# Three of GpSimd's four weight operations in each attention head wait for a named point of VectorE's order

## The reference, cut to what matters

```python
def diff_attention(...):                       # 8 heads, each with two score maps
    ...
    s = jnp.einsum('bhcqd,bhckd->bhcqk', qb, k) * scale
    s = jnp.where(mask, s, -jnp.inf)
    p = jax.nn.softmax(s, axis=-1)
    w = p[:, :, 0] - lam * p[:, :, 1]
    return jnp.einsum('bhqk,bhke->bhqe', w, vv)

def s5_branch(...):                            # linear recurrence over the positions
    ...
    _, states = lax.associative_scan(combine, (a, bu), axis=0)
    y = jnp.einsum('ghp,lbgp->blgh', c, states).real
```

## Time and profile before

| | |
|---|---|
| median of 3 runs | 2371.65 us (2371.1 to 2377.44) |
| the profiled execution, its own time | 2360.77 us |
| its span in the profile | 2359.1 us |
| mean granted TensorE clock | 0.97 |
| busy over the span | PE 93%, PEld 76%, DVE 46%, ACT 43%, POOL 35% |
| the heads' bodies 0 to 6 | from about 107 us to about 417 us |

### The profile page before, as it was taken

One profiled execution on the slowest core, in us unless ns is written; L12 is line 12 of the kernel. 1 busy time (PEld: TensorE's weight loads), 2 busy tenths in 40 slices (PEclk: granted clock), 3 DMA queues, 4 the chain that ended last, 5 costly groups with the idle time before them and its releaser, 6 DMA issues.

```text
span 2359.1 us, 31769 instructions
## 1 busy us (share of the span) xinstructions
PE 2195.1 (93%) x11292; PEld 1802.0 (76%) x11292; DVE 1089.6 (46%) x1934; ACT 1012.7 (43%) x1919; POOL 825.2 (35%) x364
## 2 busy tenths in 40 slices
PE   5988888799998997999999999999998999999997
PEld 4777777687888786888887787777777787777776
DVE  5689899525344245423225433222355543222364
ACT  5756666645234343423222433443642433444631
POOL 2422222134446322444442333333343433333342
PEclk9999999989999997999998899999999999999999
DMA  3221121132334211333332322222232322222231
GB/s 140 81 63 49 49 62 49 54 98 81 98 98 133 82 46 36 98 98 95 94 96 63 111 90 72 72 65 71 73 97 81 112 81 81 68 67 72 73 97 63
DMA packets 51741, 189.41 MB, mean 80 GB/s; under 512 B 6564, under 2 KB 7204, under 8 KB 51108
## 3 DMA queue, kind: packets, MB, share of 16 engines
q1 hardware_dynamic: 48096, 175.13, 24.9%
q10 hardware_dynamic: 2452, 6.88, 0.8%
q0 software_dynamic: 1072, 5.77, 0.6%
HBM read 185.66 MB, written 2.10 MB: 80 GB/s over the span
## 4 chain that ended last, share of the span: by engine, by line
PE 71%; DVE 13%; issue 5%; ACT 5%; DVEq 4%; POOL 2%; DMA 0%; ACTq 0%; POOLq 0%
PE bank L337 20%; PE bank L338 19%; PE bank L339 19%; PE bank L869 2%; PE bank L912 2%; POOL weight_lo L368 1%; PE bank L895 1%; DVE attention_work L1606 1%; ACT wide_region L994 1%; ACT weight_hi L363 1%; DVE wide_region L1987 1%; PE bank L411 1%; DVE work_region L1630 1%; DVEq L1572 1%; DVE wide_region L1990 1%
## 5 line engine op out<-in xcount | busy, mean ns | idle before, releaser
L368 POOL TENSOR_TENSOR weight_lo<-weight_slots,weight_hi 128x1024 fp32r<-128x1024 f32 x286 | 691.0, 2417 | 1103.2 <-ACT weight_hi L363 1103.2
L363 ACT ACTIVATE weight_hi<-weight_slots 128x1024 fp32r<-128x1024 f32 x286 | 302.6, 1059 | 825.9 <-PE bank L339 754.2
L337 PE MATMUL bank<-h_hi,weight_hi 128*128 128x512 f32 x1248 | 507.4, 407 | 20.6 <-DVE h_lo L385 12.6
L338 PE MATMUL bank<-h_lo,weight_hi 128*128 128x512 f32 x1248 | 492.1, 394 | 0.0
L339 PE MATMUL bank<-h_hi,weight_lo 128*128 128x512 f32 x1248 | 491.9, 394 | 0.0
L337 PEld LDWEIGHTS bank<-h_hi,weight_hi 128*128 128x128 f32 x1248 | 237.4, 190 | 76.0 <-DVE h_lo L385 15.2
L339 PEld LDWEIGHTS bank<-h_hi,weight_lo 128*128 128x128 f32 x1248 | 237.5, 190 | 51.6
L338 PEld LDWEIGHTS bank<-h_lo,weight_hi 128*128 128x128 f32 x1248 | 238.4, 191 | 43.9
L368 POOL TENSOR_TENSOR head_weight_lo<-weight_slots,head_weight_hi 128x1024 fp32r<-128x1024 f32 x42 | 104.3, 2485 | 293.0 <-ACT head_weight_hi L363 293.0
L337 PE MATMUL bank<-h_hi,head_weight_hi 128*128 128x512 f32 x336 | 139.3, 415 | 5.5 <-DVE h_lo L385 3.0
L338 PE MATMUL bank<-h_lo,head_weight_hi 128*128 128x512 f32 x336 | 132.8, 395 | 0.0
(11 more groups left out here) (439 smaller groups left out, 4275.9 us busy)
## 6 DMA issues: line engine op xcount, KB each, us to landing
weight_slots<-weights SPq DMA_DIRECT2D x328, 512.0 KB, 3.6
wide_region<-cmp_w ACTq DMA_DIRECT2D x2, 2048.0 KB, 8.2
v_region<-ssm_bc POOLq DMA_DIRECT2D x8, 256.0 KB, 4.8
residual<-x_in POOLq DMA_DIRECT2D x1, 2048.0 KB, 9.2
out<-normed SPq DMA_DIRECT2D x4, 512.0 KB, 2.7
residual<-x_in SPq DMA_DIRECT2D x2, 512.0 KB, 5.7
residual<-x_in ACTq DMA_DIRECT2D x2, 512.0 KB, 10.1
v_region<-mem_in POOLq DMA_DIRECT2D x1, 1024.0 KB, 5.1
```

Of the source, the lines that this page charges most:

```text
L337: pe.matmul(to, w_h[:, k, :], hi[:, k, 0:width], start=(k == 0), stop=False)
L338: pe.matmul(to, w_h[:, k, :], lo[:, k, 0:width], start=False, stop=False)
L363: act.activation(parts[0][s % 2], slot[s], ACT.Copy).then_inc(w_hi[s], 1)
L368: eng.tensor_tensor(parts[1][s % 2], slot[s], parts[0][s % 2].bitcast(F32), ALU.subtract).then_inc(w_lo[s], 1)
```

## The change: what it does

GpSimd gets three further waits in its head body. `weight_lo` of block 2 also waits until VectorE has both maxima of the second row of this head; `weight_lo` of block 0 of the next quad also waits until VectorE has generated the next head's state matrices; `weight_lo` of block 1 also waits until the next head's keys are ready. Block 3 keeps its old rule. Nothing else is changed; no other engine's program differs.

```diff
                 if last:
                     return
+                pool.wait_ge(da_max, 8 * b + 4)
                 weight_lo(pool, b + (Q_HEAD + 1), 2, W_HEADS)
                 next_input(b + 1)
                 weight_lo(pool, b + (Q_HEAD + 1), 3, W_HEADS)
+                pool.wait_ge(gen_ready, b + 2)
                 weight_lo(pool, b + (Q_HEAD + 2), 0, W_HEADS)
+                pool.wait_ge(rope_done, b + 2)
                 weight_lo(pool, b + (Q_HEAD + 2), 1, W_HEADS)
```

## The result

The changed kernel takes 2345.36 us, median of 6 runs (2341.51 to 2346.2), beside 2370.89 us for the kernel before on the same chip (2366.57 to 2377.44). The ratio is 0.9891, 95% interval 0.9879 to 0.9904: 1.1% or 25.5 us faster, where I had forecast 19.0 us and a time of 2347 to 2363 us. Its profiled execution took 2345.08 us with a span of 2343.4 us.

The account below looks back on a forecast made before the run. TensorE's waits in the heads, 5.07 us a body, were laid nearly all to VectorE, stalled by GpSimd. Six bodies at 2.9 us plus 1.55 for body 0 gave 19.0 us off 2371.65: 2352.7 us, range 2347 to 2363.

Parts of the forecast that it names:

- VectorE is late because GpSimd holds what it reads from SBUF: In the head bodies, VectorE operations reading only SBUF stall beside GpSimd's 2.4 us weight operations, taking four to six times their usual time.
- All three stalls named: In body 2: L1571 2.85 us instead of 0.69, scan L1630 2.55 instead of 0.40, L1606 2.03 instead of 0.48.
- The rival that PSUM readers are caught: L1616 and row 3's maxima would each lose 2.16 us beside GpSimd; 15 us slower in all, 2386.7; chance of slower 0.06.
- The whole-instruction rule against the earlier release: At L1621 behind block 2: VectorE let go 0.12 us before GpSimd's recorded end, or, by the skill, 0.06 us of waiting.
- Block 2, 1.40 us a body; block 0, 1.55; sum 2.9: VectorE gains 0.82 (late maxima) and 0.58 (scan's stall) at block 2, 1.55 (L1606) at block 0; 2.95, taken as 2.9.
- Waits left on TensorE: About 0.5 us before row 1's L590, and a new 1 to 1.5 us before the following L599, for ScalarE.
- 3.10 less 2.95: At row 3's last L590, TensorE could be 3.10 us earlier, VectorE's combine 2.95 us, so VectorE still sets the end.
- Body 0, 1.55, and the third wait, zero: Body 0 gains only at block 0, about 1.55 us; holding block 1 until `rope_done` gains zero, since nobody waits for it.
- The sum, 19.0: Bodies 1 to 6 at 2.9 us each, 17.4 us, plus body 0's 1.55: total 19.0 us.
- One term is left out of the sum: TensorE's clock falls at a body's end and body 7's start might vanish: 1.4 us each, up to 2.8, towards faster.
- The range: 2347 us (19.0 + 2.8 off the fastest run 2371.1, 2 us for spread) to 2363 us (late seams).

Follow-up runs that it names:

- p0_before: The kernel before, unchanged, profiled once more for a second trace; its heads end 25.0 us later than the changed kernel's.

## Why the prediction was off, by its own steps

- *VectorE is late because GpSimd holds what it reads from SBUF*: right. All three stalls named are in the trace, and each went or stayed as said. Operations with a PSUM input ran untouched beside GpSimd in the very places I had no row for (L1616, L1658). The rule of the Trainium skill ("SBUF - State Buffer", Who interferes with whom) that a VectorE instruction with at most one SBUF input, outside its 2-port modes, does not contend agrees with their 681 and 340 to 349 ns. One SBUF tensor is no safeguard by itself, though: L1606 reads one tensor and a column of scalars and was caught (1.95 us where it takes 0.41 alone). The rival that PSUM readers are caught is ruled out for these operations.
- *The whole-instruction rule against the earlier release*: L1621 started 0.09 us ahead of GpSimd's recorded end and took 0.69 us. The row speaks for the earlier release; either way the difference was under 0.1 us.
- *Block 2, 1.40 us a body; block 0, 1.55; sum 2.9*: right as a pair, 2.99 measured. The steps hold only together: alone, the first gives 0.8, because block 0 then catches L1578 for 2.17 us instead of L1606 for 1.55, and the second 1.57. 0.8 + 1.6 + the 0.6 that the second wait saves the first = 3.0.
- *Waits left on TensorE*: 0.54 and 1.52 us where I had about 0.5 and 1 to 1.5; at the last L590 0.66, where 3.10 less 2.95 gave 0.15. TensorE had half a microsecond more room than I gave it.
- *Body 0, 1.55, and the third wait, zero*: right, 1.54 and zero.
- *The sum, 19.0*: the stalls are worth 19.5 (6 x 2.99 + 1.54), so 0.5 was lost by taking 2.9 for 2.99. What failed is the step "One term is left out of the sum". I named TensorE's clock, gave it up to 2.8 us "towards a faster kernel", and then used zero for it and 2.8 only as an end of the range. Measured at a fixed place behind the heads, the mean of four traces with the old bodies is 448.4 and of four with the new ones 425.0: 23.3 us, which leaves 3.8 beside the stalls. Nine falls of 1.4 us in four traces, where the new bodies have none, are 3.2 of it; 0.6 stay open. The rest of the program is as long in both kernels (1918.8 and 1918.7 us in the mean of the same traces): nothing came from there.
- *The range*: its lower end took 19.0 and 2.8 us off 2371.1, then the fastest run of three, and 2 us for spread. Three further runs of the kernel before went down to 2366.57, so that end also stood on too few runs. The clock's term can be up to 5.5 (25.0 us at the heads' end with p0_before). With 3.8 in the sum I would have said 2349, and with 5.5 at its lower end a range from 2345 on, which would have held 2345.36 only just. The medians give 23.7 to 26.9 us over four chips; against 23.3 in the traces 0.4 to 3.6 us stay unexplained, and the rest of the program alone scatters more than that from one execution to the next (1911 to 1923 us).

## What to carry to other kernels

When an engine is held by another, look at what both operands are and where they lie, and then at the clock time of each start: here an operation of 2.4 us that starts beside four PSUM readers is free, and 1.1 us later it costs 1.7 us a body. Changing one of two such meeting points alone can shift the victim instead of freeing it, so cost them together. And when waits of more than a microsecond go away on TensorE, put the clock's falls behind them into the sum, with a count from more than one trace, not only into the range. Keep it apart as the uncertain term: falls removed by filler work alone gave nothing in the medians.

## What the runs showed of the hardware

- Falls of TensorE's clock to half follow a wait, and fill work moves them: with the waits at a body's end filled they came behind row 1's wait of 1.95 us, and with both filled none was left in bodies 1 to 6. Two traces of one kernel have them in different bodies. Each costs about 1.4 us at a body's end and 0.6 us behind row 1 (intervals of 44.57 against 43.96 us). The Trainium skill ("TensorE: Matmul & The Clock Gate", Part 1) ties the gate to how busy TensorE has lately been, which these traces bear out.
- GpSimd's 128 x 1024 subtraction takes 2.40 us whole and 3.10 us in four pieces, 0.23 us for each further start; between pieces VectorE gets in.
- The GpSimd operation that waits for `da_max` starts 0.15 us behind the end of VectorE's operation, with one register instruction between; the one that waits for `rope_done`, with none between, 0.07 us (L1589 ends at 231.61, GpSimd starts at 231.68).
